# An expert stage with ten weight slots, a written-out loop, and rank counts as accumulating products

## The reference, cut to what matters

```python
def ec_moe(u, w_router, w_gate, w_up, w_down):
    B, T, D = u.shape                                # 1, 256, 1024
    cap = (EC_CAPACITY_FACTOR * T) // N_EXPERTS      # 32 tokens for each of 16 experts
    aff = jax.nn.softmax((u @ w_router).astype(jnp.float32), axis=-1)
    gates, idx = lax.top_k(jnp.swapaxes(aff, 1, 2), cap)
    bidx = jnp.arange(B)[:, None, None]
    xs = u[bidx, idx]
    hid = jax.nn.silu(jnp.einsum('becd,edf->becf', xs, w_gate)) * jnp.einsum('becd,edf->becf', xs, w_up)
    ys = jnp.einsum('becf,efd->becd', hid, w_down) * gates[..., None].astype(u.dtype)
    return jnp.zeros_like(u).at[bidx, idx].add(ys)
```

## Time and profile before

| | |
|---|---|
| median of three runs | 3108.91 us |
| profiled execution | 3109.12 us |
| its span, first to last instruction | 3107.3 us, granted TensorE clock 0.911 |
| TensorE busy | 2600.3 us, 84% |
| VectorE, ScalarE, GpSimd busy | 577.2, 429.6, 152.2 us |
| read from HBM | 680 MB, 220 GB/s over the span |

### The profile page before, as it was taken

How to read it: one execution, slowest core, us unless ns; L and a number is a source line. 1 busy time by engine, 2 the same in 40 slices (tenths; PEclk the granted TensorE clock), 3 DMA queues, 4 the chain that set the end, 5 groups by cost and what they waited for, 6 DMA issues and landing times.

```text
span 3107.3 us, 34892 instructions
## 1 busy us (share of the span) xinstructions
PE 2600.3 (84%) x15547; PEld 1868.7 (60%) x15547; DVE 577.2 (19%) x1342; ACT 429.6 (14%) x881; POOL 152.2 (5%) x276
## 2 busy tenths in 40 slices
PE   6978878565565656655999999999999999999999
PEld 4656576121121211211788867888888886778888
DVE  2454533000000000000200442210010024331000
ACT  3333322000000000000100125210010012430100
POOL 0153340000000000000000000000000000000000
PEclk8988977887777887877999999999999999999999
DMA  7434324999999999999634333344344343434431
GB/s 234 143 82 123 99 72 165 416 416 418 417 416 418 418 416 417 418 417 415 247 134 149 136 122 136 136 136 155 129 169 142 116 168 110 163 109 149 149 122 41
DMA packets 253316, 686.52 MB, mean 221 GB/s; under 512 B 36684, under 2 KB 73965, under 8 KB 220397
## 3 DMA queue, kind: packets, MB, share of 16 engines
q1 hardware_dynamic: 248813, 683.74, 58.4%
q10 hardware_dynamic: 4352, 0.53, 0.1%
HBM read 680.04 MB, written 4.19 MB: 220 GB/s over the span
## 4 chain that ended last, share of the span: by engine, by line
PE 66%; DMA 25%; DVE 3%; SPq 2%; ACT 1%; issue 1%; POOL 1%; ACTq 0%; DVEq 0%
PE bank L1618 21%; DMA slab_ring<-in_moe_w_gate 11%; PE bank L1643 10%; DMA slab_ring<-in_moe_w_down 9%; PE bank L1744 8%; DMA slab_ring<-in_moe_w_up 5%; PE bank L1276 3%; PE bank L369 3%; PE bank L1603 3%; PE bank L1667 3%; PE bank L1687 2%; PE bank L1807 1%; PE bank L1704 1%; SPq L1201 1%; PE bank L604 1%
## 5 line engine op out<-in xcount | busy, mean ns | idle before, releaser
L1618 PE MATMUL bank<-layer_uT,slab_ring 128*128 128x256 f32 x2560 | 553.2, 379 | 0.0
L1276 PE MATMUL bank<-slab_ring,chosen_xT 128*32 128x512 f32 x2048 | 333.5, 787 | 235.0 <-DMA slab_ring<-in_moe_w_up 124.7
L1618 PEld LDWEIGHTS bank<-layer_uT,slab_ring 128*128 128x128 f32 x2560 | 486.4, 190 | 66.1
L1276 PEld LDWEIGHTS bank<-slab_ring,chosen_xT 128*32 128x32 f32 x2048 | 64.1, 128 | 487.5 <-DMA slab_ring<-in_moe_w_up 199.3
L1643 PE MATMUL bank<-ffn_hidden,slab_ring 128*128 128x256 f32 x1408 | 304.5, 379 | 0.0
L1643 PEld LDWEIGHTS bank<-ffn_hidden,slab_ring 128*128 128x128 f32 x1408 | 267.5, 190 | 36.4
L1276 PE MATMUL bank<-slab_ring,hiddenT 128*32 128x256 f32 x2048 | 173.6, 500 | 101.5 <-DMA slab_ring<-in_moe_w_down 90.4
L1744 PE MATMUL bank<-layer_uT,slab_ring 128*128 128x256 f32 x1024 | 235.4, 384 | 0.0
L1744 PEld LDWEIGHTS bank<-layer_uT,slab_ring 128*128 128x128 f32 x1024 | 191.1, 191 | 31.7 <-issue 7.7
L1276 PEld LDWEIGHTS bank<-slab_ring,hiddenT 128*32 128x32 f32 x2048 | 75.3, 139 | 194.3 <-DMA slab_ring<-in_moe_w_down 117.3
L369 PE MATMUL bank<-uT,slab_ring 128*128 128x512 f32 (+1 forms) x384 | 149.0, 544 | 1.2 <-DVE uT L844 1.2
(11 more groups left out here) (371 smaller groups left out, 2417.0 us busy)
## 6 DMA issues: line engine op xcount, KB each, us to landing
slab_ring<-in_moe_w_up SPq DMA_DIRECT2D x64, 2048.0 KB, 26.5
slab_ring<-in_moe_w_gate SPq DMA_DIRECT2D x64, 2048.0 KB, 25.3
slab_ring<-in_moe_w_down SPq DMA_DIRECT2D x64, 2048.0 KB, 26.6
slab_ring<-in_w_up SPq DMA_DIRECT2D x44, 2048.0 KB, 7.9
slab_ring<-in_w_in SPq DMA_DIRECT2D x28, 2048.0 KB, 7.8
slab_ring<-in_w_down SPq DMA_DIRECT2D x24, 1536.0 KB, 6.4
slab_ring<-in_w_mod SPq DMA_DIRECT2D x12, 2048.0 KB, 8.9
slab_ring<-in_gdn_w_in SPq DMA_DIRECT2D x32, 512.0 KB, 5.0
```

The costliest lines, as they stand in the source:

```text
L1276: ins = nc.tensor.matmul(out[32 * c:32 * c + 32, 0:cols], x, ring[:, i % NR, :].rearrange("p (k n) -> p k n", k=2 if cols == 512 else 4)[: ...
L1618: i = nc.tensor.matmul(bank[:, (j % 2) * T:(j % 2 + 1) * T], w[:, k * 512 + j * P:k * 512 + (j + 1) * P], x[:, k, :], start=(j % 2 == 0 an ...
```

## The change

- The ring has ten slots in the expert stage: six of `slab_ring` and four in a new tile over the mixer's freed tiles. The routing's tiles shrink: `late` and `early` hold four experts, and the hidden tiles lie over them. Slab n goes to slot n mod 10 and waits for slab n - 10. The layers go on with six, from slot 2.
- The loops over two turns are written out as 16 experts; nothing is gathered beyond the last.
- Comparisons of expert e wait until the products of expert e - 4 are done. Rank rows of the first six experts are made at once, the others by twos after an odd expert.
- The column sums are two products an expert, with a selector of 32 columns as weights (one column of ones, in `C_SLOT` from column 95) and the comparisons as 256 and 128 moving columns, accumulated on column group e mod 4 of bank 5. ScalarE copies the sum, TensorE turns it with two transposes.
- The first chosen tokens are evicted by pairs of chunks, in turn by VectorE and ScalarE. The opening products have 2 columns. The gated one-hots are no longer kept: `choose` multiplies when it spreads.
- The router's weights are loaded after the w_mod slab of head 2, on a semaphore of their own.

```diff
+NRE = 10
@@ sync of the mixer
-                sp.dma_start(env.wr[:], a["moe_w_router"][0].rearrange("(k p) n -> p k n", p=P)).then_inc(s_ab, 16)
...
         for h in range(1, HEADS):
             head_weights(h)
             mod_slab(h)
+            if h == 2:
+                sp.dma_start(env.wr[:], a["moe_w_router"][0].rearrange("(k p) n -> p k n", p=P)).then_inc(s_wr, 16)
@@ tiles of the expert stage
+    more = sb("slab_ring_more", [P, NRE - NR, SLAB])
+    LAG = 4
+    beats = sb("beaten_then_hidden", [P, LAG * (T + P)])
+    late = beats[:].rearrange("p (e t) -> p e t", e=LAG)[:, :, 0:T]
+    early = beats[:].rearrange("p (e t) -> p e t", e=LAG)[:, :, T:T + P]
...
+    sg = beats[:, 0:512]
+    hid = beats[:, 0:512]
+    hidT = beats[:, 512:1024].rearrange("p (c s) -> p c s", c=4)
+    ys = beats[:, 1024:1024 + GC]
@@ sync of the expert stage
             for i in range(NR if e == 0 else 0, EXPERT_SLABS):
-                sp.wait_ge(env.slab_free, EARLY_MOD + e * EXPERT_SLABS + i - NR + 1)
-                env.load(sp, i % NR, expert_slab(env, e, i))
+                n = e * EXPERT_SLABS + i
+                if n >= NRE:
+                    sp.wait_ge(env.slab_free, freed(0, n - NRE + 1))
+                src = expert_slab(env, e, i)
+                sp.dma_start(slot_of(n % NRE).rearrange("p (k n) -> p k n", k=src.shape[1]), src).then_inc(env.full[n % NRE], 16)
@@ tensor
+        for e in range(LAG + 2):
+            rank_rows(e)
         for e in range(EXPERTS):
             pe.wait_ge(pre.sem["ranks"], 2 * max(e + 1, 2))
-            nc.tensor.matmul(ps[5][:, e:e + 1], late[:, e, 0:P], const[:, C_ONES, 0:1], start=True, stop=False, skip_group_check=True)
-            nc.tensor.matmul(ps[5][:, e:e + 1], early[:, e, :], const[:, C_ONES, 0:1], start=False, stop=True, skip_group_check=True)
-            i = nc.tensor.matmul(ps[5][:, EXPERTS + e:EXPERTS + e + 1], late[:, e, P:T], const[:, C_ONES, 0:1], start=True, stop=True, skip_group_check=True)
+            q = e % 4
+            one = const[:, C_SLOT, 95 - e // 4:127 - e // 4]
+            nc.tensor.matmul(ps[5][32 * q:32 * q + 32, 0:T], one, late[:, e % LAG, :], start=(e < 4), stop=False, skip_group_check=True)
+            i = nc.tensor.matmul(ps[5][32 * q:32 * q + 32, 0:P], one, early[:, e % LAG, :], start=False, stop=(e >= EXPERTS - 4), skip_group_check=True)
+            i.then_inc(pre.next("beat_ps"), 1)
+            if e % 2 and e + LAG + 1 < EXPERTS:
+                rank_rows(e + LAG + 1)
+                rank_rows(e + LAG + 2)
+        pe.wait_ge(pre.sem["beatT"], 1)
+        for t in range(NT):
+            i = nc.tensor.transpose(ps[5][:, T + t * P:T + (t + 1) * P], lgT[:, t * P:(t + 1) * P], ident)
         i.then_inc(pre.next("rank_ps"), 1)
...
         for m in range(4):
-            nc.tensor.matmul(ps[4 + m][:, :], hid[:, 0:P], hid[:, :], start=True, stop=False, skip_group_check=True)
+            nc.tensor.matmul(ps[4 + m][:, 0:2], hid[:, 0:P], hid[:, 0:2], start=True, stop=False, skip_group_check=True)
@@ scalar
+        act.wait_ge(pre.sem["beat_ps"], EXPERTS)
+        nc.scalar.activation(lgT[:], ps[5][:, 0:T], ACT.Copy).then_inc(pre.next("beatT"), 1)
@@ vector
+            if e >= LAG:
+                dve.wait_ge(pre.sem["beat_ps"], e - LAG + 1)
@@ gpsimd
-        pool.wait_ge(env.s_h1, KC + 1)
-        nc.gpsimd.memset(hid[:], 0.0)
-        nc.gpsimd.memset(pick[:, :, EXPERTS:, :], 0.0)
-        nc.gpsimd.memset(gpick[:, :, EXPERTS:, :], 0.0).then_inc(pre.next("zeroed"), 1)
+        pool.wait_ge(pre.sem["beat_ps"], EXPERTS)
+        nc.gpsimd.memset(hid[:, 0:P], 0.0).then_inc(pre.next("zeroed"), 1)
@@ loads of the layers
+FIRST_SLOT = EXPERTS * EXPERT_SLABS % NRE
+def layer_slot(i):
+    return (FIRST_SLOT + i) % NR
     for i in range(NR):
-        sp.wait_ge(env.slab_free, SLABS_BEFORE - NR + i + 1)
-        env.load(sp, i, layer_slab(env, 0, i))
+        sp.wait_ge(env.slab_free, EARLY_MOD + EXPERTS * EXPERT_SLABS - NRE + i + 1 if i < NR - FIRST_SLOT else SLABS_BEFORE - NR + i + 1)
+        env.load(sp, layer_slot(i), layer_slab(env, 0, i))
```

More of the change, by code:

```diff
@@ L588, in shift_logits @@
         def shift_logits():
+            pe.wait_ge(s_wr, 16)
             for k in range(KC):
@@ L1156, in first_block_moe, with freed, slot_of, first_bank @@
     env.lvecs = ex.sem["lvecs"]
-    PER_TURN = EPT * EXPERT_SLABS
     ROW_BANK = (5, 6, 7, 0, 1, 2, 3, 4)
[L1160 to L1166, removed]
+    def freed(q, i):
+        return EARLY_MOD + q * EXPERT_SLABS + i
+    def slot_of(s):
+        return ring[:, s, :] if s < NR else more[:, s - NR, :]
+    def first_bank(k):
+        return ps[(6, 7, 0, 1)[k // 2]][:, (k % 2) * P:(k % 2 + 1) * P]
     def late_bank(m):
@@ L1238, in tensor, with rank_rows @@
         pe.wait_ge(pre.sem["m_aff"], 1)
-        for e in range(EXPERTS):
+        def rank_rows(e):
             b = ROW_BANK[e // 2]
@@ L1262, in tensor @@
         for k in range(KC):
[L1263 to L1264 removed]
+            i = chosen(first_bank(k), k, first)
+            if k % 2 == 1:
                 i.then_inc(pre.next("xs_ps"), 1)
         pe.wait_ge(pre.sem["zeroed"], 1)
[L1267 to L1268 removed]
+        pe.wait_ge(pre.sem["xs_out"], 2)
+        pe.wait_ge(pre.sem["xs_out_a"], 2)
         for m in range(4):
[L1270 removed]
@@ new lines, in tensor, with column_groups @@
+            nc.tensor.matmul(ps[4 + m][:, 0:2], hid[:, 0:P], hid[:, 0:2], start=True, stop=False, skip_group_check=True)
+        def column_groups(i, kk, out, x, cols, first, last):
+            for c in range(G):
+                ins = nc.tensor.matmul(out[32 * c:32 * c + 32, 0:cols], x, slot_of((q * EXPERT_SLABS + i) % NRE).rearrange("p (k n) -> p k n", k=2 if cols == 512 else 4)[:, kk, c * cols:(c + 1) * cols],
+                                       start=first, stop=last, skip_group_check=True)
+            return ins
@@ L1333, in scalar @@
                     act.wait_ge(pre.sem["m_sq"], 2 * half + t)
-                nc.scalar.activation(junk[:], ps[1 + 2 * half + t][:, :], ACT.Square, accum_out=ssq[:, half, t:t + 1]).then_inc(pre.next("m_sq"), 1)
+                nc.scalar.activation(junk, ps[1 + 2 * half + t][:, :], ACT.Square, accum_out=ssq[:, half, t:t + 1]).then_inc(pre.next("m_sq"), 1)
         act.wait_ge(pre.sem["m_self"], 1)
@@ L1574, in take @@
                 i = slab[0]
-                pe.wait_ge(env.full[i % NR], full_at(l, i))
-                return ring[:, i % NR, :]
+                pe.wait_ge(env.full[layer_slot(i)], full_at(l, i))
+                return ring[:, layer_slot(i), :]
             def used(ins):
@@ L2270, in build @@
         env.ps = [ctx.enter_context(nc.psum_tensor(f"bank{i}", [P, 512], F32)) for i in range(8)]
-        env.full = [ctx.enter_context(nc.semaphore(f"slot_full{i}")) for i in range(NR)]
+        env.full = [ctx.enter_context(nc.semaphore(f"slot_full{i}")) for i in range(NRE)]
+        env.s_out = ctx.enter_context(nc.semaphore("out_stored"))
         env.slab_free = env.ctx.enter_context(nc.semaphore("slab_free"))
@@ L2342, in constants @@
         out[:, C_SLOT, t * CAP:(t + 1) * CAP] = j[:, 0:CAP] - (T - 1 - t * P - i)
+    out[:, C_SLOT, 95] = 1
     return out
```

229 lines of the change are left out of this document (107 added, 122 removed).

## The result

The changed kernel takes 3069.15 us (median of four runs, 3065.0 to 3074.41), the kernel before 3108.76 in the same comparison. The ratio is 0.9878 [0.9860, 0.9897], so 37.9 us less, where 33.6 less and 3075.3 were forecast. Run again later beside other kernels it took 3069.67 (five runs), ratio 0.9895 [0.9878, 0.9912], 32.6 us less. As a ratio the forecast is 0.9892, inside both intervals. One of the four executions of one experiment (one column group at a time) took 3639.72 us at a mean granted clock of 0.716, where the other three had 0.912 to 0.916; it counts in the median given there and not in the ratio.

The account below looks back on a forecast made before the run. Weight transfers bound the expert stage, behind a 31.6 us idle DMA gap; TensorE bound the dense layers. Slots 20.3 + routing 9.3 + router load 4.0 = 33.6 us gave 3075.3 us, own range 3072 to 3083, 8 in 10 3069 to 3087.

Parts of the forecast that it names:

- What binds the stage: Expert stage: weight transfers bind it, after 31.6 us of idle DMA; bringing the last slab forward brings the dense layers forward equally.
- Slots, 20.3 us: Expert ring: four more slots move 4 x 5.07 = 20.3 us of slab transfers into the idle stretch during the routing.
- Routing, 9.3 us: Routing before the experts: new column sums, eviction and opening start the first expert product at 525.2, 9.3 us earlier.
- VectorE's bound of 12.8: Comparison section: with column groups side by side, VectorE's pace binds and the products end at 512.8 us.
- the series' 18.2: Comparison section: with TensorE's products and rank rows in series, switches included, it ends at 518.2 us.
- Its cap, 11.3 us: Routing gain: at most 11.3 us counts, since DMA never stops if the first expert product starts by 523.2.
- Router load, 4.0 us: Kernel start: moving the router's weights to head 2 brings w_mod forward 4.0 us, between 1.0 and 5.45.
- My least value: Router load at the start: least gain about 1.0 us, half the low-rate stretch's slack, the other half being w_ab's.
- Mode switches: Comparison products: two switches between 32-column and full weights cost 0.27 us, 1.35 us in the series sum.
- The start gave something: Answers the rival that moving the router load gains nothing at the start: 29.6 us in all, 3079.3 us; chance 0.17.
- The comparison products did not run at 1.2 GHz: Answers the rival that routing's comparison products run at 1.2 GHz throughout: gain 17.0 us, 3091.9 us; chance 0.10.
- A slab costs what it cost: Answers the rival that ten outstanding slabs slow each transfer: at 5.35 us a slab, 3126 us; chance 0.04.

## Why the prediction came out right, step by step

- **What binds the stage: right.** The gap without transfers is gone and the dense layers came forward by as much as the last down slab did. The dense part is 1619.5 us against 1619.6 predicted.
- **Slots, 20.3 us: right.** Measured 10.0 for slots seven and eight and 10.9 for nine and ten, 20.9 in all.
- **Routing, 9.3 us: mis-sized, 12.0 measured** at the last down slab (six slots against the kernel before), 12.6 at the first expert product with ten slots. The chain was right at each link, two links were too long. In times from the first rank rows: the comparison products end after 13.5 us, where I had said 15.5, between VectorE's bound of 12.8 and the series' 18.2. One group at a time costs 2.00 us a pair and the changed kernel 1.36, so the column groups do run side by side, and VectorE sets the pace; I had placed it halfway. The chosen products took 3.84 us, not 5.0, since the clock stayed at full speed from 494.7 us on. That part is not sure in every run: it fell in the profiles with six and eight slots. The eviction's tail (0.99 us) and the opening (1.02) are as said. Together 3.3 us earlier than forecast.
- **Its cap, 11.3 us: too low.** I had ended the gap where data flows again, at 537.5. But the queue that had run dry came back slowly; these are the three stages behind it in the kernel before:

```profile
537.00:538.00 1.00, 1.00 (x16) 0.31 (x12) 0.00 (x0) 0.00 (x0) 0.00 (x0) 1.00 0.73 98
538.00:539.00 1.00, 1.00 (x16) 0.34 (x12) 0.00 (x0) 0.00 (x0) 0.00 (x0) 1.00 0.74 221
539.00:540.00 1.00, 1.00 (x12) 0.26 (x8) 0.00 (x0) 0.00 (x0) 0.00 (x0) 1.00 0.91 360
```

  Their rates sum to 679, where three full ones would be 1248, so (1248 - 679) / 416 = 1.4 us more are lost. 31.6 + 1.4 = 33.0 is the whole gap, and the last down slab came forward by 32.85: the change closes all of it. Slots and routing are not two sums but one gap, and the forecast of 29.6 for both fell short by that ramp of 1.4 us and by the 2.0 us between my 9.3 and my cap.
- **Router load, 4.0 us: right in size, the way to it only in part.** 5.0 (2.5 to 7.8) by the runs. By the profiles, the first head projection is at 48.2 us on average in the three with the load at the start, and at 44.7 in the eight that have it in head 2 and are otherwise the same there: 3.5. The fourth w_mod group starts 2.4 us earlier by the same averages (38.1 and 35.7), 2.7 in the pair shown, and not the near 4 that I took from the router's issue of 5.45. Most of the rest is the group's own products, 2.00 to 3.68 us long by the clock of the run, so that 4.0 comes near 3.5 is in part luck. My least value gave half of the low rate to w_ab's rows. With w_ab in place and the router's rows gone the stage ran at 306 to 346 GB/s, so most of it was the router's.
- **Mode switches.** The price of 0.27 us for two holds: the series sum that contains it met 2.00 to 0.01. The Trainium skill, "TensorEngine Tiling (Array Packing)", Key Properties, says that a change of mode drains TensorE. The trace agrees that a switch costs time, but that does not keep the groups from running side by side between two switches: four passes of 256 and four of 128 columns took 495.52 - 494.74 = 0.78 us, where passes in a row would need 1.29.
- **The rivals.** The start gave something. The comparison products did not run at 1.2 GHz beyond the first pair, and where I put the column sums back, they did. A slab costs what it cost (416 GB/s with ten slots). The written-out loop shows nowhere in the rate of the stage, but no run has it alone, and none has the eviction by pairs alone.

Sum of the terms as measured in stretches that the mixer's noise doesn't reach: 32.85 + 3.5 = 36.4 us, between the two comparisons' 37.9 and 32.6.

Not settled: whether the last products of the stage are quicker by more than chance. Between the last down slab and the dense layers lie 5.3 to 7.3 us in all profiles, the longer ones where those products ran at a lower clock.

## What to carry to other kernels

Ahead of a stage bound by transfers, measure the whole idle gap of the DMA engines with the slow restart behind it. Each ring slot that needs nothing freed takes one slab's time off it (5.0 to 5.5 us here), and each us of the serial work that frees the first slot takes one more, until the gap is gone; past that, neither gives anything. Read such a change from an event just ahead of the stage, since a mixed stage before it can move by more than the edit is worth.

## What the runs showed of the hardware

TensorE's clock stayed low here though the engine was never idle: in the experiment with the old column sums, 48 products of one column, with rank rows between at first, ran from 493.48 to 517.8 at a granted clock of 0.50. In the changed kernel products of 256 and 128 columns in their place, alternating with the same rank rows, ran at 1.00 from the second pair on, after the same twelve rank rows at the same low clock. In the kernel before, the first of the one-column products ran at 1.00, behind the rank rows, and the clock fell within them, at about 511.2: from there they start 0.43 us apart instead of 0.22. And the clock rose while nothing but rank rows, issued as transposes, was on TensorE. In the kernel before, two stages over their passes (500.01 to 505.81), same columns as above; from 505 to 510 us it is 1.00:

```profile
503.00:504.00 1.00, 1.00 (x7) 1.00 (x6) 1.00 (x9) 0.00 (x0) 0.00 (x0) 0.50 1.00 426
504.00:505.00 1.00, 1.00 (x10) 1.00 (x9) 1.00 (x7) 0.00 (x0) 0.00 (x0) 0.83 0.95 401
```

The Trainium skill, "TensorE: Matmul & The Clock Gate", PE-mode transpose, says that full clock doesn't engage for transposes. Here nothing but f32 transposes (each one pass, where an f32 product has two) was on TensorE from 500.01 until 505.65, and the clock doubled within them, so for this form the measurement decides against the page.

SP's issue of loads can itself take 5 to 9 us behind others that are outstanding (5.58 at 13.34, 9.00 for two slabs at 484.45). Nothing else is issued in that time; it cost nothing in the second place, since SP had no other work there.
